# Row tile 3's index scores and picks moved between the query projection's chunks, and the norm rows folded into rotation tables

## The chip, the cores and the metric

One core of a Trainium2 chip runs the whole program in one launch. The metric is the device time of one execution in microseconds (us), a median over several. The core has five instruction queues: TensorE (PE, with its weight loads PEld), VectorE (DVE), ScalarE (ACT), GpSimd (POOL) and SyncE (SP), which issues most DMAs. They run independently and wait for each other by semaphores.

## The reference

Four transformer layers of width 1024 on one sequence of 512 tokens, in float32. The first two (`first_block`) are not touched by the change. The second block's two layers each do: half a SwiGLU, an RMS norm, one wide projection `w_in` (3280 columns), three mixers in parallel, an output projection, half a SwiGLU. The mixers are a sparse attention, a gated recurrence (RWKV-7) and a gated delta rule. The sparse attention is what the change is about, cut to its core:

```python
q = rope(rms_norm(q.reshape(B, L, 8, 64), q_norm), pos)      # gain per column of a head, then rotation
k = rope(rms_norm(k.reshape(B, L, 2, 64), k_norm), pos)
qi, ki = rope(qi, pos), rope(ki, pos)                         # the indexer: 8 heads, one key head
score = sum_h relu(qi_h @ ki.T) * wi_h                        # 128 queries a block, causal
_, idx = lax.top_k(score, 128)                                # L // 4 = 128 keys per query
out = softmax over the picked keys of q @ k.T * 64 ** -0.5, times v
```

## The kernel before

**Tiles.** 512 tokens are four row tiles of 128 partitions. A float32 operand is split into a high and a low part, and a product takes three matmuls (high x high, high x low, low x high). Weights come in chunks of 1024 columns by 128 rows: SP loads a chunk to `wraw`, ACT copies its high part to `wh` (L2776), POOL subtracts to get the low part `wl` (L3461). There are three `wh`/`wl` buffers, so a chunk is staged when the chunk three before it has been used. Each engine's program calls `use()` once per chunk, in the same order, and `use()` on ACT and POOL is also what stages a chunk two ahead: where it stands in ACT's program, ACT waits for TensorE to be done with an earlier chunk.

**Order of one layer of the second block** (`block2`, L1749 on PE, L2686 on DVE, L3375 on ACT, L3626 on POOL). After the norm: project the indexer's queries qi (512 columns, four chunks), then 336 columns (index key, index weights, gates; three chunks), then q (512 columns, four chunks of 24 matmuls), all with `proj_T`; then `index_heads` on PE (L1419: 16 transposes of the rotated qi, 4 of the rotated index key), then k and v (256 columns, two chunks). DVE rotates qi and the index key in its own `index_heads` (L2475; `rope`, L2186, six operations). ACT copies projections out of PSUM: q at L3390, then the transposed heads (L3167) and the index key (L3170), the squares of q (L3394), a square root of the norms' sums (`root`, L2829), gate functions, and only then `use()` for the two chunks of k.

**PSUM.** Eight banks are handed out in turn by `bank` (L742). A new user waits until the last one's result has been read. With `hold=True` a bank is left out of the turn until it is released.

**The mixer's rounds** (`mixer_rounds`, L370) are an order written out by hand: every engine walks the same loop, with lanes that each give their next piece of work. A first loop runs four times, once for each step of `heads` (on DVE, L2432: sums of squares, inverse norms, for each row tile a multiply by the norm L2445, a multiply by the gain row L2446 and a rotation, then the same for k, with a second root on ACT in between). Each of the four gives four quarters of a projected column block (`piece_F`, 24 matmuls), one step of the gates and two steps of `index`. A fifth step of `heads` transposes k and q on PE (L1410, L1416). Then come the main rounds, counted from 0: one quarter of a projected block while there are any (37 rounds), one step of `index`, one of `top`, and every other round a new attention unit (head, row tile) of the row tiles whose mask is ready. When the projections are over, the rest of the gates and then the chain of recurrence tiles (`tile_rounds`, L417) go along in the same rounds. When units and picks are done, `over()` opens more buffers and lets the next recurrence tile be made beside the current one's solve.

- `index_lane` (L332): 26 steps over 24 pairs (row tile, head), row tiles in the order 3, 2, 1. PE computes two heads' scores on every other step (L1399), ACT applies relu (L3130) into three buffers in turn, DVE adds them up with the weights (L2385, L2388), one and two steps behind. Row tile 3 has 512 columns, 2 has 384, 1 has 256.
- `top_lane` (L342): for each row tile 16 picks of eight keys (L2399 and L2400) and one step that makes the mask, once its sums are done.
- `project_lane` (L359): 13 column blocks of 4 quarters; ACT (L3144) and DVE (L2421 or L2426, L2428) work off each block.

Some units are given dummy matmuls ahead of a wait, from a table of fixed counts by unit (`WAITS`; issued at L767).

## Time and profile before

| | us |
|---|---|
| median of three runs | 3707.87 |
| lowest and highest | 3700.42, 3707.95 |
| the profiled execution: its own time | 3705.42 |
| its span | 3703.6 |
| PE busy | 3608.6 (97%) |
| DVE busy | 1938.7 (52%) |
| ACT busy | 1497.7 (40%) |
| POOL busy | 1653.4 (45%) |

The span runs from the first to the last instruction. The mean granted clock of TensorE over it is 0.992 of full speed. A busy time is the union of the engine's instructions; matmuls are pipelined, so a busy TensorE is not one at its peak. A row of a timeline has start, duration, engine, line, operation, output and input, shape and count, and in brackets the idle time before it and what ended it. "Layer 0" and "layer 1" are those of the second block.

### The profile page before, as it was taken

To read this page: it belongs to the slowest core of one execution; us is meant where nothing else is said; L and a number is where in the kernel's file an instruction comes from. 1 tells how busy PE (TensorE), PEld (TensorE's weight loads), DVE (VectorE), ACT (ScalarE), POOL (GpSimd) and SP (SyncE) were. 2 spreads that over 40 slices of the span, in tenths; PEclk is the share of its full clock that TensorE was granted. 3 is DMA by queue.
4 is the path that set the end of the run, shared out by engine and by line. 5 is a ranking of instruction groups with operands and counts; after the bars stand their busy time and mean duration, and the time that the engine had idled before them with its cause. 6 is when DMAs were issued, how large, how long until landed. Compare 5 with 4: busy or idle time off the path is not lost.

```text
span 3703.6 us, 55820 instructions
## 1 busy us (share of the span) xinstructions
PE 3608.6 (97%) x23122; PEld 2998.2 (81%) x23122; DVE 1938.7 (52%) x3397; ACT 1497.7 (40%) x2673; POOL 1653.4 (45%) x936
## 2 busy tenths in 40 slices
PE   9999999999899999999999999999999999999999
PEld 8877888888788878888767888888888876788887
DVE  2356554344645544552676635543553396655552
ACT  3444333434433343333455343334333455534332
POOL 3114566421266635664322335663666322235664
PEclk9999999999999999999999999999999999999999
DMA  4103332311243234323210034323332320012332
GB/s 129 41 29 97 114 100 66 95 52 35 67 135 100 69 101 128 101 69 89 75 46 2 3 118 123 103 64 120 104 103 75 88 57 24 3 42 90 99 103 97
DMA packets 393405, 291.95 MB, mean 79 GB/s; under 512 B 17056, under 2 KB 355904, under 8 KB 393152
## 3 DMA queue, kind: packets, MB, share of 16 engines
q1 hardware_dynamic: 387728, 284.49, 25.2%
q8 instruction: 183, 3.00, 0.3%
q10 hardware_dynamic: 5136, 2.70, 0.3%
q0 software_dynamic: 288, 1.18, 0.1%
q14 instruction: 70, 0.57, 0.0%
HBM read 286.24 MB, written 2.10 MB: 78 GB/s over the span
## 4 chain that ended last, share of the span: by engine, by line
PE 83%; DVE 10%; ACT 4%; POOL 2%; issue 1%; ACTq 0%; DMA 0%; DVEq 0%; SPq 0%; POOLq 0%
PE ps L823 13%; PE ps L824 13%; PE ps L825 13%; PE ps L1052 4%; PE ps L1053 4%; PE ps L1054 4%; PE ps L955 3%; PE ps L952 3%; PE ps L954 3%; PE ps L1080 2%; PE ps L1612 2%; PE ps L1100 2%; PE ps L1089 1%; PE ps L1162 1%; PE ps L1227 1%
## 5 line engine op out<-in xcount | busy, mean ns | idle before, releaser
L3461 POOL TENSOR_TENSOR wl<-wraw,wh 128x1024 fp32r<-128x1024 f32 (+1 forms) x424 | 1025.7, 2424 | 1555.5 <-ACT wh L2776 1552.1
L823 PE MATMUL ps<-x_T,wh 128*128 128x512 f32 (+1 forms) x2224 | 850.3, 382 | 0.0
L824 PE MATMUL ps<-x_T,wh 128*128 128x512 f32 (+1 forms) x2224 | 849.0, 382 | 0.0
L825 PE MATMUL ps<-x_T,wl 128*128 128x512 f32 (+1 forms) x2224 | 849.0, 382 | 0.0
L2776 ACT ACTIVATE wh<-wraw 128x1024 fp32r<-128x1024 f32 (+1 forms) x424 | 445.8, 1052 | 763.1 <-PE ps L825 489.9
L823 PEld LDWEIGHTS ps<-x_T,wh 128*128 128x128 f32 x2224 | 418.7, 188 | 81.4 <-POOL wl L3461 0.7
L824 PEld LDWEIGHTS ps<-x_T,wh 128*128 128x128 f32 x2224 | 418.6, 188 | 80.5 <-issue 0.5
L825 PEld LDWEIGHTS ps<-x_T,wl 128*128 128x128 f32 x2224 | 418.6, 188 | 80.4
L2060 DVE TENSOR_TENSOR scr<-scr,ps 128x512 f32<-128x512 f32 x132 | 90.6, 686 | 465.8 <-ACT scr L2931 465.8
L1052 PE MATMUL ps<-wh,h_T 128*128 128x512 f32 x672 | 262.4, 390 | 0.2
L1053 PE MATMUL ps<-wl,h_T 128*128 128x512 f32 x672 | 261.5, 389 | 0.0
L1054 PE MATMUL ps<-wh,h_T 128*128 128x512 f32 x672 | 261.5, 389 | 0.0
L3457 POOL TENSOR_TENSOR wl<-arena,wh 128x512 fp32r<-128x512 f32 x126 | 187.9, 1495 | 121.9 <-ACT wh L2773 121.8
L2106 DVE SCALAR_TENSOR_TENSOR x_tm<-ps,x_tm 128x512 f32<-128x512 f32 x224 | 154.9, 691 | 157.1 <-PE ps L955 78.3
L3457 POOL TENSOR_TENSOR wl<-mix,wh 128x512 fp32r<-128x512 f32 x150 | 212.6, 1435 | 8.2 <-ACT wh L2773 8.2
L2067 DVE TENSOR_TENSOR scr<-scr,ps 128x512 f32<-128x512 f32 x96 | 65.8, 686 | 217.1 <-PE ps L825 216.5
L1052 PEld LDWEIGHTS ps<-wh,h_T 128*128 128x128 f32 x672 | 126.1, 188 | 29.9 <-POOL wl L3457 2.6
L1054 PEld LDWEIGHTS ps<-wh,h_T 128*128 128x128 f32 x672 | 126.2, 188 | 26.1
L1053 PEld LDWEIGHTS ps<-wl,h_T 128*128 128x128 f32 x672 | 126.2, 188 | 25.8
L2773 ACT ACTIVATE wh<-mix 128x512 fp32r<-128x512 f32 x150 | 91.8, 624 | 125.0 <-PE ps L825 47.8
L952 PE MATMUL ps<-wh,h_T 128*128 128x512 f32 x352 | 138.0, 392 | 0.0
L955 PE MATMUL ps<-wh,h_T 128*128 128x512 f32 x352 | 137.1, 390 | 0.0
(822 smaller groups left out, 6876.7 us busy)
## 6 DMA issues: line engine op xcount, KB each, us to landing
wraw<-in_ffn_w_gate_dram SPq DMA_DIRECT2D x88, 512.0 KB, 3.9
wraw<-in_ffn_w_up_dram SPq DMA_DIRECT2D x88, 512.0 KB, 3.9
wraw<-in_w_in_dram SPq DMA_DIRECT2D x82, 512.0 KB, 3.7
wraw<-in_w_gate_dram SPq DMA_DIRECT2D x44, 512.0 KB, 3.9
wraw<-in_w_up_dram SPq DMA_DIRECT2D x44, 512.0 KB, 3.9
mix<-in_ffn_w_down_dram SPq DMA_DIRECT2D x20, 1024.0 KB, 6.8
arena<-in_ffn_w_down_dram SPq DMA_DIRECT2D x12, 1024.0 KB, 6.4
wraw<-in_ffn_w_down_dram SPq DMA_DIRECT2D x24, 512.0 KB, 3.7
```

The source lines that it names most:

```text
L823: mm(b[:, t0:t1], wh[:, k, :], xTh[:, k, t0:t1], k == 0, False)
L824: mm(b[:, t0:t1], wh[:, k, :], xTl[:, k, t0:t1], False, False)
L825: ins = mm(b[:, t0:t1], wl[:, k, :], xTh[:, k, t0:t1], False, k == 7)
L952: mm(o, lh(k, j), wh[:, q, :], k == 0, False)
L955: ins = mm(o, ll(k, j), wh[:, q, :], False, k == K - 1 and not apart)
L1052: mm(b[:, :], hF[:, q, 0, m, t], wh[:, u, :], first and q == 0, False)
L1053: mm(b[:, :], hF[:, q, 0, m, t], wl[:, u, :], False, False)
L1054: ins = mm(b[:, :], hF[:, q, 1, m, t], wh[:, u, :], False, q == pairs - 1)
L2106: return stt(xs, b[:, :], -0.5 if minus else 0.5, xs, ALU.mult, ALU.add)
L2776: copy(hl_of(w)[0], raw_of(w)).then_inc(*s.sig("w", "hi", w))
L3457: tt(wl[:, u, :], fast_src(prod, q), wh[:, u, :].bitcast(F32), ALU.subtract).then_inc(*g.sig("w", "lo", w, u))
L3461: tt(wl, raw_of(w), wh.bitcast(F32), ALU.subtract).then_inc(*g.sig("w", "lo", w))
```

## The change

1. `early_rounds` replaces the plain q, `index_heads`, k order on every engine: one q chunk, `index_heads`, then four index steps, a chunk, four index steps, a chunk, two index steps and two picks, a chunk (q's last), four picks, a chunk (k), four picks, a chunk (k). q and k are projected by `chunks_T`, which gives a chunk at a time and holds its four banks. The lanes `index` and `top` are then handed on to `mixer_rounds`, which takes one step of `top` in each of its four first rounds as well.
2. ACT copies q out inside these rounds. Its wait for the index key's rotation, the squares of q and all behind them come after the last chunk's `use()`.
3. POOL makes eight tables after its last `use()` of the projection: cosine and sine times the two halves of the q and the k gain row, into arena columns that are free there. DVE's rotation of q and k multiplies by these and drops the five multiplies by gain rows (four for q, one for k). DVE waits for the tables before the first rotation of q.

```diff
+def early_rounds(proj, heads, index, top):
+    next(proj)
+    heads()
+    for scores, picks in ((4, 0), (4, 0), (2, 2), (0, 4), (0, 4)):
+        for _ in range(scores):
+            next(index)
+        for _ in range(picks):
+            next(top)
+        next(proj)
...
 def mixer_rounds(...):
     while next(heads, "end") != "end":
...
         for _ in range(2):
             next(index)
+        next(top)
...
+            def chunks_T(*widths):
+                for n in widths:
+                    ws, kk = [], WCH // n
+                    for c in range(8 // kk):
+                        ws.append(use())
+                        if c == 0:
+                            last = ws[0] + 8 // kk - 1
+                            bks = [bank(("Tm", last, j), ("ev", last, j), hold=True) for j in range(NT)]
+                            for _, free in bks:
+                                pe.wait_ge(*free)
...
+                        ins.then_inc(*pe.sig("w", "used", ws[c]))
+                        if k == 7:
+                            for j in range(NT):
+                                held.discard(book.bank[("Tm", last, j)])
+                        yield
...
 (PE, block2)
                 proj_T(8, 336, xh, xl)
-                proj_T(8, 512, xh, xl)
-                index_heads(l)
-                proj_T(8, 256, xh, xl)
...
+                index = index_lane(0, summed, lambda i, h: index_sum(l, i, h))
+                top = top_lane(summed, masks, nothing, nothing, nothing)
+                early_rounds(chunks_T(512, 256), lambda: index_heads(l), index, top)
...
 (DVE, heads)
-                    step(tt(qx, qx, bc(rows["qn"].unsqueeze(1), [P, 8, 64]), ALU.mult))
-                    rotate(qx, j)
+                    tm = [...]
+                    v.wait_ge(*at("dsa", "turn", l))
+                    turn(qx[:, :, 0:32], qx[:, :, 32:64],
+                         [bc(turn_c[0][:, a, j, :].unsqueeze(1), [P, 8, 32]) for a in range(4)], tm)
...
-                step(tt(kx, kx, bc(rows["kn"].unsqueeze(1), [P, 8, 64]), ALU.mult))
...
 (DVE, block2)
-                index_heads(l)
+                early_rounds(rests(6), partial(index_heads, l), index, top)
...
 (ACT)
+            def chunks(l):
+                for _ in range(3):
+                    use()
+                    yield
+                w = use()
+                for j in range(NT):
+                    s.wait_ge(*at("w", "used", w))
+                    copy(qtm2[:, j, :], psum_of("Tm", w, j)[:, :]).then_inc(*s.sig("ev", w, j))
+                yield
+                for _ in range(2):
+                    use()
+                    yield
...
+                early_rounds(chunks(l), partial(index_heads, l), index, top)
                 s.wait_ge(*at("dsa", "ropek", l))
-                w = use(tiles_of(8, 512))
...
-                index_heads(l)
...
-                w = use(tiles_of(8, 256))
+                w = where["w_in_2", l, 512]
...
 (POOL, after use(13))
+                early_rounds(rests(6), nothing, index, top)
+                g.wait_ge(*at("pb2", l))
+                for k, gain in enumerate((rows["qn"], rows["kn"])):
+                    for a, (tab, o) in enumerate(((rope_c, 0), (rope_s, 32), (rope_s, 0), (rope_c, 32))):
+                        ins = tt(turn_c[k][:, a], tab, bc(gain[:, o:o + 32].unsqueeze(1), [P, 4, 32]), ALU.mult)
+                ins.then_inc(*g.sig("dsa", "turn", l))
```

## Rows read from the trace of the kernel before

**Rows 1.** The page: TensorE's busy time, and the chain that ended last by engine

```profile
PE 3608.6 (97%) x23122; PEld 2998.2 (81%) x23122; DVE 1938.7 (52%) x3397; ACT 1497.7 (40%) x2673; POOL 1653.4 (45%) x936
...
PE 83%; DVE 10%; ACT 4%; POOL 2%; issue 1%; ACTq 0%; DMA 0%; DVEq 0%; SPq 0%; POOLq 0%
```

**Rows 2.** Windows by stage, layer 0 then layer 1: us, engines' busy time (instructions), clock

```profile
1808.50:1835.50 27.00, 26.90 (x112) 18.94 (x112) 25.41 (x43) 13.40 (x29) 7.53 (x3) 1.00 0.29 79
1835.50:1843.50 8.00, 4.20 (x29) 2.96 (x27) 6.02 (x7) 7.96 (x15) 2.39 (x2) 1.00 0.24 66
1843.50:1938.00 94.50, 91.14 (x432) 65.99 (x431) 74.81 (x187) 49.37 (x110) 21.64 (x10) 1.00 0.17 51
1938.00:2000.60 62.60, 60.54 (x630) 45.99 (x629) 40.39 (x137) 34.58 (x99) 13.26 (x11) 0.95 0.01 2
2000.60:2021.20 20.60, 18.93 (x323) 15.53 (x317) 13.62 (x33) 13.02 (x30) 9.78 (x10) 1.00 0.01 2
...
2998.80:3006.80 8.00, 5.73 (x29) 4.26 (x27) 6.00 (x7) 7.89 (x14) 2.34 (x1) 0.79 0.25 68
3006.80:3101.00 94.20, 90.70 (x431) 65.77 (x429) 74.81 (x187) 49.23 (x110) 21.54 (x9) 1.00 0.17 51
3101.00:3163.00 62.00, 58.40 (x576) 42.64 (x574) 40.36 (x137) 34.83 (x99) 12.65 (x10) 1.00 0.01 2
```

**Rows 3.** Timeline of TensorE, layer 0's q projection and key transposes: start, us, idle before

```profile
1771.76 0.39 PE L952 MATMUL ps<-wh,x_T 128*128 128x512 f32 x1
...
1793.53 1.91 PE L1426 MATMUL ps<-cr,mix 128*128 128x128 f32 x16
1795.28 0.60 PE L1432 MATMUL ps<-cr,arena 128*64 128x128 f32 x4
1796.54 0.35 PE L952 MATMUL ps<-wh,x_T 128*128 128x256 f32 x1 [0.66 <-ACT arena L3167]
```

**Rows 4.** Timeline of ACT, the same stretch to the second root

```profile
1793.73 2.07 ACT L3390 ACTIVATE arena<-ps 128x512 f32<-128x512 f32 x4 [4.39 <-PE ps L955]
...
1796.60 1.22 ACT L3170 ACTIVATE arena<-ps 64x512 f32<-64x512 f32 x2
1797.84 2.20 ACT L3394 ACTIVATE scr<-arena 128x512 f32<-128x512 f32 x4
...
1829.43 0.21 ACT L2829 ACTIVATE arena<-arena 128x8 f32<-128x8 f32 x1 [4.50 <-DVE arena L1864]
```

**Rows 5.** Timeline of VectorE, rotations, gain multiplies and lengthened operations

```profile
1775.18 0.28 DVE L2193 TENSOR_TENSOR arena<-scr 128x128 f32<-128x128 f32 x1
1794.67 1.50 DVE L2486 COPY arena<-ps 128x512 f32<-128x512 f32 x2 [19.20 <-PE ps L1426]
...
1803.19 0.69 DVE L2446 TENSOR_TENSOR arena<-arena,pbuf 128x512 f32<-128x512 f32 x1
...
1806.18 2.78 DVE L2445 TENSOR_TENSOR arena<-arena 128x512 f32<-128x512 f32 x1
...
1823.72 2.41 DVE L2449 SCALAR_TENSOR_TENSOR arena<-arena 128x16 f32<-128x16 f32 x1
```

**Rows 6.** GpSimd: a weight operation in its timeline, and a group of lines by form

```profile
1864.75 2.41 POOL L3461 TENSOR_TENSOR wl<-wraw,wh 128x1024 fp32r<-128x1024 f32 x1 [8.43 <-ACT wh L2776]
...
L3501 POOL TENSOR_TENSOR arena<-arena,pbuf 128x256 f32<-128x256 f32 x8 | 6.3, 784 | 66.6 <-ACT mix L3189 61.9 <-DVE spare L2599 3.2 <-PE ps L1470 1.5
```

**Rows 7.** Timeline of TensorE, layer 0, from the last `heads` round to the first main round

```profile
1834.51 1.13 PE L1399 MATMUL ps<-arena 64*128 64x512 f32 x4
...
1838.70 1.53 PE L1416 MATMUL ps<-cr,arena 128*128 128x128 f32 x12 [2.04 <-DVE arena L2421]
...
1842.71 0.92 PE L1399 MATMUL ps<-arena 64*128 64x384 f32 x4 [1.35 <-DVE arena L2472]
```

**Rows 8.** Timeline of VectorE, one pick of a main round in layer 0

```profile
1863.85 0.69 DVE L2399 MAX8 cols<-arena 128x8 f32<-128x512 f32 x1
...
1864.65 0.68 DVE L2400 MATCH_REPLACE8 arena<-cols,arena 128x512 f32<-128x512 f32 x1
```

More of the change, by code:

```diff
@@ L600, in build_program @@
         hbT = cut(0, 3584, "p (a t) -> p a t", a=7)
+        turn_c = [cut(1024 + 512 * k, 512, "p (a t n) -> p a t n", a=4, t=4) for k in range(2)]
         gT = cut(3584, 3072, "p (a t) -> p a t", a=6)
@@ L1763, in over @@
                     stock.open()
-                mixer_rounds(heads(l), lambda h, i: unit3(l, ("dsa", h, i)),
-                             index_lane(0, summed, lambda i, h: index_sum(l, i, h)),
-                             top_lane(summed, masks, nothing, nothing, nothing),
+                mixer_rounds(heads(l), lambda h, i: unit3(l, ("dsa", h, i)), index, top,
                              project_lane(piece_F, last_F), gates(l),
@@ L2186, in rope, with turn @@
             def rope(x1, x2, cs, sn, tmp, *key):
+                turn(x1, x2, (cs, sn, sn, cs), tmp, *key)
+            def turn(x1, x2, by, tmp, *key):
                 a, b_, c_, d_ = tmp
-                tt(a, x1, cs, ALU.mult)
-                tt(b_, x2, sn, ALU.mult)
-                tt(c_, x1, sn, ALU.mult)
-                step(tt(d_, x2, cs, ALU.mult))
+                tt(a, x1, by[0], ALU.mult)
+                tt(b_, x2, by[1], ALU.mult)
+                tt(c_, x1, by[2], ALU.mult)
+                step(tt(d_, x2, by[3], ALU.mult))
                 tt(x1, a, b_, ALU.subtract)
@@ L2691, in block2 @@
                 use(tiles_of(8, 336))
-                index_heads(l)
+                masks, summed, stock = set(), set(), Stock(l)
+                index = index_lane(2, summed, partial(index_sum, l))
+                top = top_lane(summed, masks, partial(top_first, l), partial(top_step, l), partial(top_last, l))
+                early_rounds(rests(6), partial(index_heads, l), index, top)
                 use(tiles_of(8, 512))
@@ L2709, in over @@
                     v.wait_ge(*v.own())
-                mixer_rounds(heads(l), lambda h, i: unit3(l, ("dsa", h, i)),
-                             index_lane(2, summed, partial(index_sum, l)),
-                             top_lane(summed, masks, partial(top_first, l), partial(top_step, l), partial(top_last, l)),
+                mixer_rounds(heads(l), lambda h, i: unit3(l, ("dsa", h, i)), index, top,
                              project_lane(nothing, partial(project, l)), rests(16),
@@ L3373, in lifts @@
                 small_dma(lora[64:128, :], A["rwkv_g_up_2"][l]).then_inc(*s.dma("lora", l))
+            def chunks(l):
[3 more added lines that the diff above has]
+                w = use()
+                for j in range(NT):
+                    s.wait_ge(*at("w", "used", w))
[4 more added lines that the diff above has]
+                    yield
             def block2(l):
@@ L3385, in block2 @@
                     copy(gz[:, j, :], b[:, 72:336]).then_inc(*s.sig("ev", w, j))
+                masks, summed, stock = set(), set(), Stock(l)
+                index = index_lane(1, summed, partial(index_sum, l))
+                top = top_lane(summed, masks, nothing, nothing, nothing)
+                early_rounds(chunks(l), partial(index_heads, l), index, top)
                 s.wait_ge(*at("dsa", "ropek", l))
-                w = use(tiles_of(8, 512))
-                for j in range(NT):
-                    s.wait_ge(*at("w", "used", w))
-                    copy(qtm2[:, j, :], psum_of("Tm", w, j)[:, :]).then_inc(*s.sig("ev", w, j))
-                index_heads(l)
+                w = where["w_in_2", l, 0]
                 for j in range(NT):
@@ L3412, in over @@
                     stock.open()
-                mixer_rounds(heads(l), lambda h, i: unit3(l, ("dsa", h, i)),
-                             index_lane(1, summed, partial(index_sum, l)),
-                             top_lane(summed, masks, nothing, nothing, nothing),
+                mixer_rounds(heads(l), lambda h, i: unit3(l, ("dsa", h, i)), index, top,
                              project_lane(nothing, partial(project, l)), gates(l),
@@ L3631, in block2 @@
                 masks, summed, stock = set(), set(), Stock(l)
+                index = index_lane(0, summed, nothing)
+                top = top_lane(summed, masks, nothing, nothing, nothing)
+                early_rounds(rests(6), nothing, index, top)
[4 more added lines that the diff above has]
+                ins.then_inc(*g.sig("dsa", "turn", l))
                 def over():
@@ L3640, in project @@
                         stage(wat[0] + AHEAD + 1)
-                mixer_rounds(rests(4), lambda h, i: rests(4), index_lane(0, summed, nothing),
-                             top_lane(summed, masks, nothing, nothing, nothing),
+                mixer_rounds(rests(4), lambda h, i: rests(4), index, top,
                              project_lane(nothing, project), rests(16),
```

15 lines of the change are left out of this document (11 added, 4 removed).

## The prediction

> **What bounds the kernel now.** I read the page first [rows 1]: TensorE is busy 97% of the span and holds 83% of the chain that ended last, VectorE 10%. So a change pays only where TensorE stands idle, or works at half clock. The change touches one stage, once per layer of the second block (from about 1757 us in layer 0). The windows of that stage [rows 2] show where TensorE is idle: 0.1 us of 27 while the four rounds of `heads` run, 3.8 us of 8 where they hand over to the main rounds, 3.4 us of 94.5 in the main rounds with projection pieces, 2.1 us of 62.6 in the rounds without them, 1.7 us of 20.6 while the first recurrence tile is being solved beside the second's making. Layer 1 has 2.3 us of 8 at clock 0.79, 3.5 and 3.6. VectorE is full in the `heads` rounds (25.4 of 27) and 79% full in the main rounds. About 11 us a layer is thus the most that a better order can give back. The 19.2 us in which VectorE waits for TensorE's transposes [rows 5] is the room that the change fills; it is idle time of an engine that bounds nothing there.
>
> **The change part by part, layer 0; layer 1 repeats it.**
>
> *Rounds.* TensorE's instructions stay the same, only their order changes. Before, `heads` gives 8 of the 26 index steps and no pick. Row tile 3 is then picked in main rounds 1 to 17, tile 2 in 18 to 34, tile 1 in 35 to 51, and tile 1's eight units start in rounds 52 to 59; the loop ends at round 63. After, 10 index steps and 10 picks are done early and 4 more picks in `heads`, so the masks come at rounds 2, 19 and 36, the units become what is in order (rounds 47 to 54), and the loop ends at 58. The projection still ends at 37 and the chain of recurrence tiles still starts at 41. The second tile may be made only after the loop: before that is chain round 24, and its 17 steps, two a round, end at 32, while tile 0 is solved at 28; after, they start at 19 and end at 27. Four chain rounds go, but no work goes with them.
>
> *Index work moved.* Five pairs of score matmuls move ahead of `heads`: four of 1.1 us (512 columns) and one of 0.9 (384), 5.3 us [rows 7]. The four pairs in `heads` become narrower, 1.1 us less together, and what is left for the main rounds is 3 pairs instead of 8: four of 0.9 and one narrower go, 4.0 to 4.2 us. Moved, it nets to zero.
>
> *New wait for the transposed index keys.* Before, 12 us of k projection stood between these transposes and their first reader. Now the first pair follows them at once, and needs the key copy: ACT's copies ended 2.5 us after the first key transpose (1795.28 to 1797.82) [rows 3, 4], and the transposes themselves take 0.6, so TensorE stands about 1.6 us (bounds 0.8, if the two copies come sooner because q is no longer copied first, and 2.5). The transposes themselves come after one q chunk (5.4 us) and their rotations end 3.7 us after the q projection starts [rows 3, 5], so these don't wait.
>
> *Banks.* Four of eight banks are held through q's chunks; the index pairs rotate through the other four. By my count k's four banks are then one index bank and three of q's. k must wait for ACT's copies of q tiles 0 to 2, three quarters of 2.07 us plus the signal [rows 4]: 1.75 us where 0.66 is lost now [rows 3], so +1.1 (bounds 0 and 1.8).
>
> *VectorE's chain to the hand-over.* This is the term that decides. ACT squares q before it asks for k's weights now; in the new order both k chunks' `use` come first, and the second stages the weights that need k's first chunk done. That is at 1771.76 + 21.8 (96 matmuls of q, up to the first transpose at 1793.53) + 2.4 (transposes) + 1.6 + 5.1 (the five pairs, less where one runs into the next) + 1.75 + 6.0 (half of k's 1796.54 to 1808.50) = 1810.4. One weight copy more, and ACT's squares start near 1811.4, against 1797.84: +13.6 us [rows 3, 4]. Behind them on VectorE stand, up to the second root that ACT waits for at 1829.43:
> - four gain multiplies of 0.7 are gone: -2.8 [rows 5].
> - two picks of about 1.5 us each: +3.0 [rows 8]; four score sums instead of two: +0.9, an estimate from operations of 512 columns at 0.69 and these being narrower [rows 5].
> - the rotation tables: eight GpSimd operations of 128x128 come behind two weight operations. 128x256 took 0.78 us, 128x1024 2.4 [rows 6], so 0.4 to 0.5 each, ready near 1818, when VectorE wants them at 1816.3: +1.7 (bounds 0 and 5).
> - GpSimd's weight operations: a gain multiply of VectorE took 2.78 us beside one, 0.69 alone [rows 5, 6]. Four operations are lengthened so in the passage, 2.1 to 2.2 us each, 8.6 in all (first and last in [rows 5]); in the new order two of the weight operations fall on picks, whose rows show no such lengthening (0.68 us beside GpSimd's 2.41) [rows 6, 8], so about 2.6 us remains: -6.0 (bounds 0 and -8.6).
>
> Sum: 13.6 - 2.8 + 3.9 + 1.7 - 6.0 = +10.4 us (bounds 5 and 16). ACT's gate functions, its next projection act and VectorE's sum of it all stand behind that root, and the q transposes wait for the last of these (2.04 us now) [rows 7], so the first main round moves from 1843.56 to about 1854.0. Less the 4.0 us of index work already done, TensorE is 6.4 us behind per layer, the 1.6 and 1.1 included.
>
> On the tables there is a rule that speaks against the change. The Trainium skill ("SBUF — State Buffer") says that a VectorE operation with two SBUF inputs and a GpSimd operation that reads SBUF exclude each other for the whole instruction. The trace agrees (2.78 against 0.69 us); by that rule each of the eight table operations could hold up one multiply, 8 x 0.45 = 3.6 us a layer where I take 1.7, and the sum would be 4 us higher over both layers.
>
> *What comes back.* In the main rounds VectorE has less to do: sums 3 pairs narrower and fewer, and picks of 384 and 256 columns instead of 512 early on. I let 2.4 of the 3.4 us idle of TensorE there vanish [rows 2]. In the two stages behind it no pick runs beside the recurrence, and four rounds less: 1.4 of 3.8 us. The dummy matmuls that keep the clock up are the same in number, so the waits they cover give nothing back. Together -3.8.
>
> *Sum.* (6.4 - 3.8) x 2 = +5.2 us on the profiled execution's 3705.4, so 3710.6; the median of the runs shown is 2.45 us above that execution, so **3713**. Within 0.2% (7.4 us, about what a measurement of this kernel can tell from no change).
>
> **The rivals.**
>
> *A, faster (0.25): the hand-over does not slip and the rounds pay.* If ACT's squares or the tables are not what VectorE waits for (more GpSimd lengthenings vanish, the shift is 5 us and not 10.4), TensorE is only 1 us behind at the first main round, and then gets back the idle of the three stages, 7.2 us at most, and the half-clock stretch inside 1938 to 2000.6 (mean 0.95, 3.1 us) [rows 2]. Taking 6 of these: -5 a layer, 3698. For it: VectorE is 94% busy in `heads`, and the change does take work from that stretch. Against: it also puts work in.
>
> *B, slower (0.33): the wait at the hand-over grows and stays.* Place: the q transposes after `heads`, behind VectorE's sum of the third projected column block. Price: 6.4 us a layer, nothing recovered because the main rounds are TensorE's anyway (96% busy), and a longer idle there lets the clock fall, as it already did in layer 1 (mean 0.79 over 8 us, 1.7 us lost) [rows 2]: (6.4 + 1.7) x 2 = +16, 3724. It decides from the point at which VectorE reaches the second root more than about 8 us later than now. For it: every step of the sum above. Against: VectorE is 79% busy in the main rounds, so it can catch up.
>
> *C (inside the forecast): the early picks don't come early.* The sums follow ACT's relu copies, which now share ACT's queue with weight copies that wait for chunks. If picks slip by a few rounds the masks are still ready before the units; nothing changes on TensorE.
>
> **How the numbers follow.** Forecast with C 0.42, own range 3704 to 3721; A 0.25, centred on 3698; B 0.33, centred on 3724. Of the forecast a tenth lies beyond +0.2%, of B nine tenths: slower 0.04 + 0.30 = 0.34. Of A three quarters is faster by over 0.2%, of the forecast next to nothing: 0.20 with a little for the latter. Same is the rest, 0.46. The range reaches to where a third of A (0.08) and a third of B (0.11) are left out: 3694 to 3728.
>
> **What would show it.** In the changed profile: TensorE waits about 1.6 us for ACT at the first index pair, and 1.7 us for ACT's q copy at k's first matmul; the idle of 19.2 us on VectorE is gone, filled with picks; the first reduce of q's squares starts about 14 us later, the multiply by the rotation table waits for GpSimd 1 to 2 us; TensorE's idle at the hand-over is 6 to 9 us instead of 3.8; its idle in the main rounds falls to about 1 us; the loop ends five rounds earlier. I am wrong if the hand-over's idle does not grow (then A), or if the main rounds keep their idle (then B).

## The result, and the profile after

The changed kernel takes 3750.72 us (median of four runs, 3746.31 to 3753.76) against 3704.14 for the kernel before (four runs): ratio 1.0128, 95% interval 1.0116 to 1.014. It is 46.6 us slower, far outside the range of 3694 to 3728. The profiled execution took 3752.09 us, span 3750.2.

From the page of the changed kernel, the engines' busy time [rows 1]:

```profile
PE 3627.8 (97%) x23122; PEld 3012.6 (80%) x23122; DVE 1943.3 (52%) x3387; ACT 1500.3 (40%) x2673; POOL 1661.6 (44%) x952
```

TensorE has the same number of instructions as before and is still 97% busy. The loss of 46.6 us of span has two parts: it is idle for 3750.2 - 3627.8 = 122.4 us where it was 95.0 (+27.4), and busy for 19.2 us more with the same instructions. The second part goes with the clock: the mean granted clock is 0.985 instead of 0.992, which over the span is 56 us of full speed not granted instead of 30. All runs below are read by these two numbers, **idle** (span minus busy) and **clock loss** (one minus the mean granted clock, times the span).

**Up to the hand-over the forecast of the delay held.** Timelines of the changed kernel in layer 0: TensorE, ACT, VectorE, GpSimd. TensorE starts q's projection at 1774.43 instead of 1771.76, so 2.67 us of every shift are from ahead of the change.

```profile
1783.60 1.99 PE L1439 MATMUL ps<-arena 64*128 64x512 f32 x8 [1.37 <-ACT arena L3213]
...
1807.27 0.36 PE L817 MATMUL ps<-wh,x_T 128*128 128x256 f32 x1 [1.87 <-ACT arena L3425]
```

```profile
1814.77 1.06 ACT L2819 ACTIVATE wh<-wraw 128x1024 fp32r<-128x1024 f32 x1 [6.33 <-PE ps L819]
1815.73 2.18 ACT L3450 ACTIVATE scr<-arena 128x512 f32<-128x512 f32 x4
...
1843.78 0.21 ACT L2872 ACTIVATE arena<-arena 128x8 f32<-128x8 f32 x1 [7.62 <-DVE arena L1902]
```

```profile
1816.38 2.85 DVE L2478 TENSOR_REDUCE arena<-scr 128x8 f32<-128x512 f32 x4 [2.04 <-ACT scr L3450]
...
1822.24 0.42 DVE L2230 TENSOR_TENSOR scr<-arena 128x256 f32<-128x256 f32 x1 [0.84 <-POOL arena L3692]
```

```profile
1818.27 3.87 POOL L3692 TENSOR_TENSOR arena<-con,pbuf 128x128 f32<-128x128 f32 x8
```

TensorE waits 1.37 us for the index key and 1.87 for q's copies; the squares move by 17.9 - 2.7 = 15.2 us [rows 4], VectorE waits 0.84 us for the tables, the second root moves by 11.7 us, and the first main round by 12.4 (1858.59 against 1843.56, TensorE's first matmul behind the scores in [rows 7]). One sign failed: TensorE's idle from k's transposes to the main rounds was to be 6 to 9 us and is 3.5 (1850.14 to 1858.59). The delay lies ahead of it: 3.2 us in the two waits above, 3.3 us idle in the `heads` rounds (three waits of 0.7 to 1.4 us for VectorE and ACT), the index scores that moved ahead, and a clock of 0.70 for 5.7 us behind the wait for q's copies.

**Behind the hand-over it fell.** Windows of the changed kernel: main rounds with projection pieces, then from their end to the first solve of recurrence tile 0; and the same two of the kernel before (its second window is cut at the solve, 1984.7, so that both end at the same step of the recurrence):

```profile
1858.60:1962.30 103.70, 95.56 (x432) 70.77 (x431) 65.95 (x185) 46.47 (x103) 20.51 (x9) 0.95 0.16 46
1962.30:2017.30 55.00, 48.54 (x324) 35.57 (x323) 22.64 (x79) 32.19 (x88) 12.64 (x10) 0.91 0.00 1
```

```profile
1938.00:1984.70 46.70, 44.65 (x318) 31.86 (x318) 34.92 (x119) 29.41 (x79) 12.54 (x10) 1.00 0.00 1
```

The first window takes 103.7 us where it took 94.5 [rows 2], although 4 us of index work had left it; the second 55.0 instead of 46.7. Clock 0.95 and 0.91 instead of 1.00 and 1.00, idle 8.1 and 6.5 us instead of 3.4 and 2.1. VectorE has 8.9 us less to do in the first and it helps nothing. The greatest sum in the changed kernel's list of TensorE's waits (what waits, what ends the wait; us in total, times, the longest one):

```profile
PE ps L1129 <- ACT scr L3222: 23.0, 17, 2.9
```

The same entry of the kernel before:

```profile
PE ps L1089 <- ACT scr L3179: 7.4, 11, 1.2
```

The transposes of a unit's probabilities wait for ACT's exponential: 23.0 us instead of 7.4. One such wait in the changed kernel, TensorE and ACT around unit 6 of row tile 3:

```profile
1935.35 2.44 PE L781 MATMUL ps<-cr 128*128 128x384 f32 x13
1937.63 0.60 PE L1129 MATMUL ps<-cr,scr 128*128 128x128 f32 x4
...
1945.55 0.66 PE L1129 MATMUL ps<-cr,scr 128*128 128x128 f32 x4 [2.40 <-ACT scr L3222]
```

```profile
1939.71 0.68 ACT L3187 ACTIVATE arena<-ps,small 128x512 f32<-128x512 f32 x1
1940.40 1.28 ACT L3251 ACT_TABLE_LOAD   x1
1941.70 1.67 ACT L3251 ACTIVATE arena<-arena 128x512 f32<-128x512 f32 x3
1943.39 1.28 ACT L3222 ACT_TABLE_LOAD   x1
1944.68 0.72 ACT L3222 ACTIVATE scr<-scr,small 128x512 f32<-128x512 f32 x1
```

ACT is late with this exponential because three SiLU operations and two table loads (4.2 us) stand ahead of it. In the kernel before the same batch of the gates falls to unit 5:

```profile
1917.67 1.28 ACT L3208 ACT_TABLE_LOAD   x1
1918.97 1.68 ACT L3208 ACTIVATE arena<-arena 128x512 f32<-128x512 f32 x3
1920.66 1.28 ACT L3179 ACT_TABLE_LOAD   x1
```

```profile
1920.24 2.44 PE L767 MATMUL ps<-cr 128*128 128x384 f32 x13
1922.82 0.66 PE L1089 MATMUL ps<-cr,scr 128*128 128x128 f32 x4
```

Here 13 dummy matmuls (`WAITS[("dsa", 5, 3)]`) fill the wait and TensorE goes on 0.14 us behind them. The dummies are counted by unit, the SiLU batch by round. The change makes masks ready earlier, so the units of row tile 3 start in rounds 16 to 30 instead of 18 to 32, those of tile 2 in 32 to 46 instead of 36 to 50, those of tile 1 from 47 instead of 52. Unit 5 now comes before the batch and pays 2.44 us for dummies that cover nothing; unit 6 waits 2.40 us with no cover. The clock falls behind some such waits and not behind others: in layer 0 TensorE runs at half clock for 3.4 us from 1907.2, behind a wait of 1.69 us of unit 0, and from 1989.1, behind one of 2.35, but at full clock behind the wait of unit 6 shown here.

By layers: layer 0 is 12.4 us behind at the first main round, 21.6 at the end of the projection, 29.9 at the first solve, and gets 12.6 back behind it, so that layer 1 begins 17.3 us later against layer 0's begin than before (VectorE's first index rotations: 1757.81 and 2921.16 before, 1760.49 and 2941.09 after). The other 26.6 us (46.6 - 2.7 - 17.3) are lost from there on: layer 1 is 12.3 us behind at its first main round and 31.1 at its first solve, and only 4.5 come back. The figures at the solve are not all delay: by then the changed kernel has issued 24 unit matmuls more (its units start earlier), about 4 us of work, an estimate from its rows (four products 0.66 us, three transposes 0.55, two scores 0.70).

### The profile page after: what moved, and what is told of

Read it like the earlier page. It is cut to its first block and busy times, and to the rows that moved or that the text cites. A ratio compares the mean times of both kernels' runs of the same rounds, so it can differ in the third digit from the quotient of the medians.

```text
span 3750.2 us, 55818 instructions
## 1 busy us (share of the span) xinstructions
PE 3627.8 (97%) x23122; PEld 3012.6 (80%) x23122; DVE 1943.3 (52%) x3387; ACT 1500.3 (40%) x2673; POOL 1661.6 (44%) x952
## 5 line engine op out<-in xcount | busy, mean ns | idle before, releaser
L2816 ACT ACTIVATE wh<-mix 128x512 fp32r<-128x512 f32 x150 | 91.8, 624 | 125.0 <-PE ps L865 47.8
```

## The experiments

A cover is a group of dummy matmuls that fills a wait. Theory 1: the units' rounds moved off their covers. Theory 2: the late hand-over is the whole loss. Rival 3: the tables. Every kernel ran beside runs of the kernel before; the last column compares the medians, and the interval around such a difference is some 4 to 8 us to either side. Idle and clock loss are those of the one profiled execution, which can lie off the median: that of g1 took 3690.6 us against a median of 3697.9, that of m1 3711.9 against 3718.7.

| run | us (before) | ratio, interval | idle, clock loss | against before |
|---|---|---|---|---|
| before | | | 95, 30 | |
| changed | 3750.7 (3704.1) | 1.0128, 1.0116-1.014 | 122, 56 | +46.6 |
| s1_starts | 3727.8 (3702.3) | 1.0067, 1.0052-1.0082 | 108, 41 | +25.5 |
| p1_haste | 3738.4 (3702.3) | 1.0098, 1.0083-1.0113 | 110, 56 | +36.1 |
| t1_tables | 3713.8 (3702.3) | 1.0033, 1.002-1.0045 | 99, 37 | +11.5 |
| o1_order | 3749.8 (3702.3) | 1.0131, 1.0116-1.0147 | 118, 60 | +47.5 |
| w0_nodummies | 3744.3 (3702.7) | 1.0114, 1.0098-1.013 | 123, 75 | +41.6 |
| b0_nodummies | 3710.2 (3702.7) | 1.0019, 1.0009-1.0028 | 111, 44 | +7.5 |
| q1_squares | 3746.4 (3702.7) | 1.0115, 1.01-1.013 | 120, 56 | +43.7 |
| g1_tabearly | 3697.9 (3702.7) | 0.9988, 0.9977-0.9999 | 92, 22 | -4.8 |
| w1_moved | 3728.7 (3701.6) | 1.0071, 1.0055-1.0088 | 107, 52 | +27.0 |
| p2_moved | 3736.4 (3701.6) | 1.0089, 1.0074-1.0104 | 96, 75 | +34.7 |
| h2_all | 3716.3 (3701.6) | 1.0039, 1.0024-1.0054 | 106, 33 | +14.6 |
| h1_latepicks | 3722.3 (3701.6) | 1.0054, 1.0039-1.0069 | 105, 41 | +20.6 |
| k1_qfirst | 3724.6 (3703.6) | 1.0059, 1.0044-1.0074 | 110, 41 | +21.0 |
| m1_mended | 3718.7 (3703.6) | 1.0045, 1.0028-1.0062 | 102, 41 | +15.2 |
| m2_clock | 3732.8 (3703.6) | 1.0078, 1.0057-1.0099 | 100, 56 | +29.2 |
| k2_qfirst | 3716.1 (3700.7) | 1.0039, 1.0025-1.0052 | 102, 37 | +15.4 |
| b1_misplaced | 3717.3 (3700.7) | 1.0046, 1.003-1.0063 | 105, 41 | +16.7 |
| h3_root | 3716.1 (3704.1) | 1.0032, 1.0021-1.0043 | 104, 37 | +12.0 |

### The units' rounds and their covers

**s1_starts**: the changed kernel, units in their old rounds.

```diff
+STARTS = {0: 0, 3: 18, 2: 36, 1: 52}
-        if todo and (n % 2 == 0 or ...) and todo[0][1] in masks:
+        if todo and (n % 2 == 0 or ...) and todo[0][1] in masks and n >= STARTS[todo[0][1]]:
```

> The changed kernel, with the softmax units of row tiles 3, 2 and 1 held back to the rounds in which they started before (18, 36 and 52, where the change lets them start in 16, 32 and 47). Picks, scores and tables stay as changed. Theory 1 (the rounds of the units): against the projection's pieces, which take four rounds a chunk, the units' exponentials now fall two or four rounds earlier, so that they meet the rounds in which ScalarE and VectorE first have to finish a projected chunk, and the dummy matmuls that were counted for certain units cover nothing: then most of what is lost behind the hand-over comes back, 10 to 17 us a layer, 3715 to 3730 us, TensorE's waits for the exponential fall from 23 us to about 8, and the half-clock stretches behind the hand-over go. Theory 2 (the late hand-over alone is the loss, and the rounds behind it suffer because everything starts late): 3743 to 3753. Rival 3 (the clock, whatever the units do): waits fall but the half-clock stretches stay, 3735 to 3745.

**p1_haste**: the kernel before, units in the new rounds.

```diff
+HASTE = (4, 8, 20, 40, 41)
-        if top and next(top, "end") == "end":
-            top = None
+        for _ in range(1 + (n in HASTE)):
+            if top and next(top, "end") == "end":
+                top = None
```

> The kernel before, with five picks done a round earlier (two picks instead of one in main rounds 4, 8, 20, 40 and 41), so that the units start in exactly the rounds of the changed kernel (16, 32, 47) and nothing else of the change is in it. Theory 1 (the rounds of the units): 10 to 17 us a layer slower, 3724 to 3738 us, with waits of TensorE for the exponential at the same units as in the changed kernel. Theory 2 (late hand-over): 3699 to 3709, no change.

Both came out as theory 1 says: holding the units back gives 21 us of the 46.6 back (46.6 - 25.5), and moving them in the kernel before costs 36.1. Theory 2 alone had 3743 to 3753 and no change. With the units held back the waits for the exponential are 10.4 us in all, and the rounds behind the projection, up to the first solve, take 45 us at full clock, where the changed kernel takes 55 at 0.91:

```profile
1953.10:1998.10 45.00, 43.97 (x318) 31.84 (x317) 22.87 (x75) 29.34 (x79) 12.34 (x10) 1.00 0.00 1
```

In p1, part of the 36 is the doubled picks' own: in rounds 4 and 8 the exponential behind them was 2.4 and 1.4 us late.

**w0_nodummies** and **b0_nodummies**: the changed kernel and the kernel before, each without 65 of 74 dummies a layer.

```diff
-... ("dsa", 0, 3): 6, ("dsa", 5, 3): 13, ("dsa", 0, 2): 8, ("dsa", 3, 2): 21, ("dsa", 1, 2): 4, ("dsa", 5, 2): 8, ("dsa", 6, 2): 5}
+... ("dsa", 4, 0): 5, ("dsa", 6, 0): 4}
```

> The changed kernel without the dummy matmuls of the units of row tiles 3 and 2 (65 of 74 a layer; those of row tile 0 stay). 13 of them took 2.44 us at full clock, so 65 are 12 us of TensorE a layer. Theory 1a (the dummies cover nothing any more: they stood ahead of the units that met ScalarE's SiLU batches, and now stand two and four rounds beside them): their time comes back, less what they did cover at units 0 of tile 3 and by chance, and less the clock: 8 to 20 us faster than the changed kernel over both layers, 3730 to 3743. Theory 1b (they still keep the clock up, wherever they stand): the half-clock stretches grow by as much as the dummies cost, 3746 to 3756.

> The kernel before, without the same 65 dummy matmuls a layer. Theory 1a: here they stand in waits that are there anyway (3.8 of the 12 us at the most are not), and keep the clock: 2 us faster to 14 us slower than before, 3700 to 3716. If dummies cost their time here too (rival): 3680 to 3690.

The same edit brings the changed kernel 5.0 us nearer to the kernel before (3744.3, between the two theories; its interval overlaps that of the changed kernel) and makes the kernel before 7.5 us slower. So the covers are worth some 12 us less after the change than before it, of which only the 7.5 stand clear of the noise. TensorE's bare waits stand in the timelines of these two runs. Of b0 (the kernel before, no dummies):

```profile
1889.05 0.66 PE L1087 MATMUL ps<-cr,scr 128*128 128x128 f32 x4 [1.61 <-ACT scr L3177]
1895.82 0.63 PE L1087 MATMUL ps<-cr,scr 128*128 128x128 f32 x4 [1.19 <-ACT scr L3177]
1919.84 0.66 PE L1087 MATMUL ps<-cr,scr 128*128 128x128 f32 x4 [2.42 <-ACT scr L3177]
1940.84 0.89 PE L1087 MATMUL ps<-cr,scr 128*128 128x128 f32 x3 [1.94 <-ACT scr L3177]
1958.31 0.90 PE L1087 MATMUL ps<-cr,scr 128*128 128x128 f32 x3 [3.79 <-ACT scr L3177]
```

These are units 0, 1 and 5 of tile 3 and 0 and 3 of tile 2: apart from unit 1 the ones that the table gives 6, 13, 8 and 21 dummies. Of w0 (the changed kernel, no dummies):

```profile
1903.65 0.66 PE L1127 MATMUL ps<-cr,scr 128*128 128x128 f32 x4 [2.75 <-ACT scr L3220]
1917.24 0.66 PE L1127 MATMUL ps<-cr,scr 128*128 128x128 f32 x4 [1.09 <-ACT scr L3220]
1941.29 0.66 PE L1127 MATMUL ps<-cr,scr 128*128 128x128 f32 x4 [2.42 <-ACT scr L3220]
...
1981.27 0.90 PE L1127 MATMUL ps<-cr,scr 128*128 128x128 f32 x3 [2.40 <-ACT scr L3220]
```

Units 0, 2 and 6 of tile 3, 5 of tile 2.

**w1_moved**: the changed kernel with covers there; **p2_moved**: the hastened kernel with the same. The new table has 55 dummies a layer in place of 65; the ten fewer are worth 1.9 us a layer at full clock (13 took 2.44 us).

```diff
+... ("dsa", 0, 3): 15, ("dsa", 2, 3): 6, ("dsa", 6, 3): 13, ("dsa", 5, 2): 21}
```

> The changed kernel with its dummy matmuls set where its own trace has the waits: without dummies these stand at units 0, 2 and 6 of tile 3 (2.75, 1.09 and 2.42 us) and 5 of tile 2 (about 4), so 15, 6, 13 and 21 dummies go there, and those at 5 of tile 3 and 0, 1, 3 and 6 of tile 2 go. Theory 1a (the covers stand at the wrong units): the waits that remain there vanish, the clock holds better, 3730 to 3740. Rival (the covers matter only by their own length): as without dummies, 3743 to 3747.

> The kernel before with five picks hastened, so that its units start in the rounds of the changed kernel (3738 so), and with the dummies moved to the units that wait there, as in the changed kernel with moved covers. Theory 1a: most of the 36 us comes back except what the doubled picks themselves hold up in rounds 4 and 8 (some 3 us a layer) and the clock there: 3712 to 3725. If the rounds cost for another reason than the covers (rival): 3728 to 3738.

In the changed kernel 20 us come back (46.6 - 27.0), up to 4 of them by the fewer dummies, and 3728.7 is a little better than expected; the waits for the exponential fall from 23.0 to 7.1 us. p2 missed: it is 1.4 us nearer to the kernel before than p1, in the range of its rival. Its idle fell from 110 to 96 us, all that was to be had (95 before), but its clock loss rose from 56 to 75. So in the hastened kernel the moved covers close the waits and win nothing. A window of p2, in the rounds behind the projection:

```profile
1975.00:2012.00 37.00, 34.69 (x218) 25.16 (x216) 13.98 (x48) 14.20 (x46) 3.26 (x4) 0.53 0.00 1
```

TensorE is busy 34.7 of 37 us at nearly half clock (1.2 GHz). In layer 1 there is such a stretch of 47.8 us from 3151.2. The moved table has no dummies left in these rounds but one group; w1 has the same table and the same rounds, and its mean clock from the end of the projection to the first solve is 0.89 in layer 0 and 0.93 in layer 1, where p2's is 0.66 and 0.72. What makes that difference stays open.

**b1_misplaced** tests the covers in the kernel before alone, by one unit each.

```diff
-("dsa", 5, 3): 13 ... ("dsa", 3, 2): 21
+("dsa", 4, 3): 13 ... ("dsa", 4, 2): 21
```

> The kernel before with nothing changed but two groups of dummies, each one unit away: the 13 of unit 5 of tile 3 go to unit 4, the 21 of unit 3 of tile 2 to unit 4. Theory 1a (a dummy is free inside a wait and costs its time elsewhere): per layer 2.4 and 3.8 us of waits open up where they stood, and the dummies take 2.4 and 3.8 us where they go, of which the clock takes some back or adds: 8 to 20 us slower, 3711 to 3723. Rival (their place matters little, as the clock looks over a longer stretch): within 4 us of before.

16.7 us slower, inside what theory 1 said (8 to 20). TensorE's timeline has both prices, the dummies at unit 4 and the wait at unit 5 (and 3.79 us at unit 3 of tile 2):

```profile
1915.60 2.45 PE L767 MATMUL ps<-cr 128*128 128x384 f32 x13
1917.89 0.60 PE L1089 MATMUL ps<-cr,scr 128*128 128x128 f32 x4
1925.81 0.65 PE L1089 MATMUL ps<-cr,scr 128*128 128x128 f32 x4 [2.41 <-ACT scr L3179]
```

### The tables

**t1_tables**: the kernel before with the tables alone. **o1_order**: the changed kernel without them. **g1_tabearly**: t1 with the eight GpSimd operations ahead of the weights.

```diff
 (POOL, block2, g1_tabearly)
                 stage(wat[0] + AHEAD)
+                g.wait_ge(*at("pb2", l))
+                for k, gain in enumerate((rows["qn"], rows["kn"])):
+                    ...
                 use(13)
```

> The kernel before, with the norms' rows put into the rotation tables and nothing else of the change. By my sum: four gain multiplies of 0.7 us less before the hand-over and one more for k (which takes longer), against a wait for the eight GpSimd operations, which come behind the same weight operations as in the changed kernel while VectorE asks for them some 14 us earlier. Between -3 us a layer (tables ready in time: 3698) and +6 us a layer (VectorE waits for them: 3716); I take 3703. If the tables were what makes the change slow, this one would be above 3730.

> The changed kernel without its tables: the norms' rows are multiplied on VectorE as before, the order is the new one. Theories 1 and 2 both: four more multiplies of 0.7 us and one less table wait of 0.8 us before the hand-over, 2 to 3 us a layer slower than the changed kernel, 3750 to 3757. If the tables were what makes the change slow (rival): below 3735.

> The kernel before with the rotation tables that carry the norms' rows, as in the run of the tables alone (+11 us), but the eight GpSimd operations stand ahead of GpSimd's weights of the projection instead of behind them, so that VectorE finds them ready (it waited for them until 1814.0, and 3.1 us of gain multiplies are gone). Theory: the hand-over comes 3 us earlier than in the kernel before instead of 4 us later, TensorE waits that much less there: 3692 to 3702. If the tables cost something else than this wait (rival): 3706 or more.

Alone the tables cost 11.5 us. VectorE's timeline in t1: it reaches the first rotation and stands until GpSimd, which comes to the tables behind 4.8 us of weights, has made them:

```profile
1814.00 0.43 DVE L2193 TENSOR_TENSOR scr<-arena 128x256 f32<-128x256 f32 x1 [11.06 <-POOL arena L3642]
```

From the first index rotation to k's transposes at the hand-over t1 takes 82.9 us, the kernel before 77.8, g1 77.7; VectorE comes to the reduce for k after 74.5, 70.7 and 65.7 us, and TensorE to its first main round after 90.3, 85.8 and 83.0. In the new order the tables are worth nothing either way (3749.8 without, 3750.7 with), because VectorE asks for them later. Made early they are the one part of the change that pays, if little: **g1 is 4.8 us faster than the kernel before** (ten runs, 3690.62 to 3702.9; interval 0.9977 to 0.9999, only just clear of no change). The trace bears the size out: at the first solve g1 is 2.6 us ahead in layer 0 and 2.3 in layer 1. The profiled execution as a whole (span 3688.8) is well below its median, so that its idle, 3 us lower, and its clock loss, 8 lower, say too much: 5.7 us of its gain lie ahead of the first index rotation, a point at which the other profiled runs are between 3.0 us ahead of the kernel before and 2.7 behind it.

### The order at the hand-over

**q1_squares**: the changed kernel, with the four squares behind q's copies in ACT's `chunks`, ahead of k's `use()`. **h2_all**: s1, q1 and g1's place of the tables together. **h1_latepicks**: h2 without the ten picks between the chunks.

```diff
 (h1_latepicks)
-    for scores, picks in ((4, 0), (4, 0), (2, 2), (0, 4), (0, 4)):
+    for scores, picks in ((4, 0), (4, 0), (2, 0), (0, 0), (0, 0)):
```

> The changed kernel, with ScalarE's squares of q right behind its copies of q, before k's weights are asked for, as it was before the change. VectorE's early picks end at 1813.8, and it then waits 2.0 us for the squares, so the hand-over comes 2 to 3 us earlier a layer, and the rounds behind it lose what they lose: 3744 to 3750. If the order on ScalarE were the whole cause of the late hand-over (rival): 3730 or less.

> The changed kernel with its units in the old rounds (3727.8 so), ScalarE's squares right behind q's copies, and the rotation tables made before GpSimd's weights of the projection. The early picks stay. The squares were worth 1 us a layer, the tables' wait 0.8: 3721 to 3726.

> As the run with the old rounds, early squares and early tables, but the ten picks between the chunks are left to the later rounds (four come in the four rounds of the hand-over, the rest in the main rounds, all masks still ready in time). Theory 2a (the early picks fill VectorE until 1813.8, and q's squares, ready near 1809, queue behind them): the hand-over comes 5 to 8 us earlier a layer, 3708 to 3716. Rival 2b (q's projection is late by the index scores ahead of it, and the picks only fill the wait): no change, 3720 to 3726.

The squares alone give 3 us by the differences to before, which is inside the noise, and the trace shows no gain at the hand-over: in q1 ACT squares 8.4 us earlier and VectorE multiplies q 1.3 us earlier, but k's transposes come 88.3 us after the first index rotation in both. h2 is 11 us better than s1, more than expected: its clock loss is 33 instead of 41. Taking the early picks away does not help: h1 is 6 us slower than h2, although k's transposes come 0.6 us earlier in it (86.7 against 87.4). So the early picks are not what holds the hand-over, and theory 2a fell. What holds it in h1 is in its timeline of ACT: the root of q's norms stands behind the weight copy for k, which waits for TensorE, and VectorE waits 3.0 us for it.

```profile
1807.28 2.21 ACT L3430 ACTIVATE scr<-arena 128x512 f32<-128x512 f32 x4
1809.36 1.07 ACT L2820 ACTIVATE wh<-wraw 128x1024 fp32r<-128x1024 f32 x1
1814.70 1.06 ACT L2820 ACTIVATE wh<-wraw 128x1024 fp32r<-128x1024 f32 x1 [4.26 <-PE ps L820]
1815.66 0.21 ACT L2873 ACTIVATE arena<-arena 128x32 f32<-128x32 f32 x1
```

**h3_root**: h1 with `root(rr2[:, 0:32], ...)` right behind the squares.

> As the run with late picks (3722.3), with ScalarE's square root of q's norms right behind the squares instead of behind k's two weight copies. Theory 2c (q's norm is held by ScalarE's queue, in which k's weights wait for TensorE): VectorE's multiply comes near 52 us after the first index rotation instead of 57.9, the hand-over 3 to 6 us earlier a layer, less up to 1 us for k's weight copy, which now waits for VectorE's reduces: 3711 to 3718. Rival (VectorE or TensorE is late for another reason): 3719 or more.

VectorE's first multiply of q comes 51.5 us after the first index rotation instead of 57.9, as expected, and the kernel is 8.6 us nearer to before. But k's transposes come only 1.1 us earlier (85.6 against 86.7; the kernel before 77.8): VectorE itself is full from there on (busy for 31.2 of the 34.1 us up to k's transposes).

**k1_qfirst** and **k2_qfirst**: h2 with q's four chunks first again and only eight scores early; k2 has ACT's squares behind its copies of the transposed heads and one chunk of k ahead of the scores. As built, k1 has four scores ahead of k's first chunk and four between its two chunks, and k2 has all eight between them; the expectations place them later.

```diff
-    next(proj)
+    for _ in range(4):
+        next(proj)
     heads()
-    for scores, picks in ((4, 0), (4, 0), (2, 2), (0, 4), (0, 4)):
+    for scores, picks in ((4, 0), (4, 0)):          (k2: next(proj), four scores, then ((4, 0),))
```

> Old rounds, early squares and early tables as in the run that gave 3716.3, but q's four chunks go ahead of the index transposes again, eight index scores go between the two chunks of k, and the early picks are left to the later rounds. Theory 2b (what is left of the loss is q's projection, late by the 9.3 us of transposes, key wait and score pairs that the change puts ahead of it): VectorE finds q's squares near 1798 again, the hand-over comes as in the kernel before or 3 us earlier, less eight sums of 0.6 us, 3696 to 3706. If the index work ahead of the hand-over costs by itself, wherever it stands (rival): 3712 to 3718.

> Old rounds and early tables, q's four chunks and then the index transposes as in the kernel before, ScalarE's copies and squares in their old order; of the change only eight index scores stay early, four between k's two chunks and four behind them, with no early pick. Theory 2b (the loss at the hand-over is that q and its squares are late): like the kernel before with early tables, 3697.9, and up to 3 us a layer slower for the eight sums that VectorE then does ahead of the rotations: 3696 to 3705. Rival (index work ahead of the hand-over costs by itself): 3712 or more.

Theory 2b fell as it was put: with q as early as before, the hand-over is late all the same (the first main round of layer 0 by 11.7 us in k1, by 9.0 in k2). k1 is even slower than its rival said: once a layer TensorE waits 4.1 us there for the key copies, which stand behind the squares. In k2 the squares are done in time, but VectorE's queue has the early sums ahead of its reduces, and these wait 8.07 us for scores that TensorE has behind a chunk of k:

```profile
1804.65 0.49 DVE L2432 TENSOR_SCALAR arena<-scr,arena 128x512 f32<-128x512 f32 x1 [8.07 <-ACT scr L3178]
```

Its reduces of q's squares start 53.7 us after the first rotation instead of 40.7. In all five variants of this section with old rounds and early tables (h2, h1, h3, k1, k2) index sums stand ahead of `heads`, k's transposes are 8 to 13 us later than before, and 12 to 21 us remain. In k2 and h1 it is an in-order queue that holds q's norm; what the remainder is made of is not shown. Sums behind the reduces were not tried: there are three relu buffers, so scores can't run ahead of sums.

### Can the new order be mended?

**m1_mended**: the changed kernel in its new rounds with early squares, early tables and moved covers. **m2_clock**: with 25 dummies a layer more, (0, 2): 8, (1, 2): 4, (3, 2): 8, (6, 2): 5.

> The changed kernel (new order, new rounds) with early squares, early tables, and the dummies moved to the units that wait. The moved covers gave 22 us, squares and tables 11 us on the kernel with old rounds: if the two add up, 3714 to 3720. If the sparse rounds behind the projection then lose the clock, as they did for 37 us at a stretch in the hastened kernel with moved covers (rival): 3728 to 3740.

> As the mended kernel above, with 25 dummies a layer more, in the rounds behind the projection (8, 4, 8 and 5 at units 0, 1, 3 and 6 of tile 2), where nothing has to be waited for. Their price is 4.6 us a layer at full clock. Theory 3 (those rounds are too sparse to hold the clock, and dummies there pay by the clock alone): the half-clock stretches between rounds 32 and 54 shrink, and the time stays within 5 us of the mended kernel, 3708 to 3720. Rival (dummies pay only inside waits): 9 us slower than it.

m1 is 31 us better than the changed kernel, against the kernel before, and 15 behind it. m2 is 14 us slower than m1 by the medians, where the dummies' own time is 9.4: they did not hold the clock. The executions of m1 have mean clocks of 0.984 to 0.989, those of m2 0.984 to 0.988, so the losses of 41 and 56 overstate the difference, but no gain is seen. Theory 3 fell for these places.

## Why the prediction was wrong

- **The delays priced ahead of the hand-over held.** Key copy 1.6 against 1.37 us, k's banks 1.75 against 1.87, tables 1.7 against 0.84, squares +13.6 against +15.2, hand-over chain +10.4 against +11.7 at the root and +12.4 at the first main round. Less the 4.0 of index work done, 8.4 a layer instead of 6.4: this term missed by 4 us in all. Only the place of the idle was wrong (3.5 us at the hand-over, 6 to 9 forecast). The 3.6 us by the rule on the tables did not come: the eight operations took 0.48 us each, and beside them one multiply of VectorE took 0.87 instead of 0.69.
- **The step that failed is "What comes back", -3.8 a layer**, and in it this sentence: "The dummy matmuls that keep the clock up are the same in number, so the waits they cover give nothing back." Same in number, but counted by unit, while the waits that they cover come by round. I had worked out the new rounds of the masks (2, 19 and 36) and of tile 1's units (47 to 54), and used them only to count how many rounds go. The runs put a price on it: 21 us by holding the units back, 20 by moving the covers (up to 4 of them by fewer dummies), some 12 from the difference between the two kernels without dummies, and 36 in a kernel that has the new rounds and five doubled picks. These overlap and don't add up. In the last one the moved covers win only 1.4 us, so the new rounds have a price beside the waits, in the clock, whose cause stays open. In all, the term came out at +13.6 a layer instead of -3.8 ((46.6 - 2.7 - 2 x 8.4) / 2).
- **VectorE's relief was worth nothing in the main rounds.** VectorE did get 8.9 us less work in them, and I let 2.4 us of TensorE's idle vanish for it. Even in s1, with the covers in place, that idle is 5.4 us (1857.76 to 1953.08) where it was 3.4. In the changed kernel TensorE waited there for a chain across three engines (scores, maximum, exponential, transposes), in which ACT's own queue was late, not VectorE's load.
- **Rival B** had the direction and one mechanism of two: the hand-over wait grows, the clock falls. Its 16 us are near what was left with rounds, squares and tables put right (14.6 in h2, 15.2 in m1), but that is luck: B was priced with the late squares and tables in it, and the run that has those and only the rounds put right, s1, is 25.5 us behind. It lacked the covers.
- **Behind the projection** I let 1.4 us a layer come back for the four chain rounds. From the first solve on, 12.6 came back in layer 0 and 4.5 in layer 1, about 4 of each being unit work done ahead (24 matmuls more by the first solve in both). But 3.0 and 7.3 came back in layer 0 of s1 and h2 as well, where the loop ends as late as before. So the runs don't show what the four rounds are worth.
- **The tables** by themselves were slower by 11.5 us and were not priced alone. In the sum I took 1.7 us of wait for them, right for the new order only.

The Trainium skill ("ScalarE: Activation LUTs", What ACT_TABLE_LOAD costs) gives 1283 ns for a table load and another 1380 ns of drain for every switch. The loads in the changed kernel's trace take 1.28 us; the exponential behind the SiLU batch starts 1.29 us after its load did, so no such drain is seen here. The batch takes 4.2 us by the rows, where an estimate by the page's two figures would be 7.0 (2 x 2.66 + 1.67).

## What to carry to other kernels

A filler that is counted for one place in a written-out schedule is part of the schedule: after any edit that moves work by a round, list the waits without fillers, and set the fillers again before you judge the edit. When work moves between in-order queues, follow what each engine has queued ahead of the next critical operation (a root behind a weight copy, reduces behind sums), since idle time on an engine is room only for what its queue can reach. Price each part of a change alone where it can stand alone: here one of two parts paid, by little, and only in another place.

## What was not expected of the hardware

TensorE ran a stretch of 37 us at a granted clock of 0.53 while 34.7 us of it were busy, in p2, in the rounds of small transposes and 64-column products behind the projection; and 25 dummies a layer in the same kind of rounds did not raise the mean clock of m2 over m1's. It can be held there: the kernel before (its window above) and s1 have these rounds at 1.00 up to the first solve, with the dummies inside their waits. Without the dummies the kernel before has them at 0.83 in layer 0 and at 0.90 in layer 1:

```profile
1938.40:1989.40 51.00, 43.90 (x274) 28.63 (x272) 33.83 (x119) 29.85 (x79) 12.11 (x10) 0.83 0.00 1
```

A VectorE operation on 16 columns took 2.26 us in k2 where its neighbours took 0.17, as the lengthened ones in [rows 5]. A weight operation of GpSimd ran beside it, from 1809.37 for 2.40 us:

```profile
1809.35 0.17 DVE L2748 TENSOR_TENSOR arena<-arena,pbuf 128x16 f32<-128x16 f32 x1
1809.55 2.26 DVE L2749 TENSOR_SCALAR arena<-arena 128x16 f32<-128x16 f32 x1
```
